# 128 of v's 1024 columns summed on VectorE for the first tile, h kept in two buffers, and the sample's selection and a second staging rearranged

## What is computed

```python
    h = x + mix
    hn = rmsnorm(h, norm_ffn_w)
    y = h + peer(hn.reshape(bsz * t, D_MODEL), peer_w_q, peer_sub_keys, peer_u, peer_v).reshape(bsz, t, D_MODEL)
...
        sv, si = lax.top_k(sc, PEER_TOPK)
        cand = sv[:, :, 0, :, None] + sv[:, :, 1, None, :]
...
        fv, fi = lax.top_k(cand.reshape(PEER_BLOCK, PEER_HEADS, PEER_TOPK * PEER_TOPK), PEER_TOPK)
...
        gate = jax.nn.softmax(fv, axis=-1)
        ue = u[eidx]
        ve = v[eidx]
        act = jax.nn.gelu(jnp.einsum('thkd,td->thk', ue, xb).astype(F32), approximate=False)
        return jnp.einsum('thk,thkd->td', (gate * act).astype(xb.dtype), ve)
```

## Time and profile before

| | |
|---|---|
| median of 3 runs | 3275.91 us |
| the profiled execution: own time | 3276.45 us |
| its span | 3274.7 us |
| TensorE busy | 2923.6 us (89%) |
| VectorE busy | 2114.2 us (65%) |
| GpSimd busy | 2074.2 us (63%) |
| ScalarE busy | 1532.2 us (47%) |
| moved by DMA | 1226.83 MB, mean 375 GB/s |
| the DMA engines' share | 0.9 or more in all but five of the 40 slices |
| of it, gathers (software queue) | 1121.46 MB |

### The profile page before, as it was taken

How to read it: one execution, slowest core, us unless ns; L and a number is a source line. 1 busy time by engine, 2 the same in 40 slices (tenths; PEclk the granted TensorE clock), 3 DMA queues, 4 the chain that set the end, 5 groups by cost and what they waited for, 6 DMA issues and landing times. The chain is left out here.

```text
span 3274.7 us, 31544 instructions
## 1 busy us (share of the span) xinstructions
PE 2923.6 (89%) x8213; PEld 1379.7 (42%) x8213; DVE 2114.2 (65%) x4852; ACT 1532.2 (47%) x4160; POOL 2074.2 (63%) x2162
## 2 busy tenths in 40 slices
PE   7998999879998999799988998899888997889966
PEld 6854544335443544354433443344334342343221
DVE  2465556656577656865667657875787477655684
ACT  3415642356336643475336643674358333633333
POOL 1105574766667676767667776777677776657675
PEclk9999999999999999999999999999999999989999
DMA  8518999999999999999999999999999999999998
GB/s 287 191 60 327 363 409 336 383 408 402 400 371 408 395 410 393 399 409 400 409 371 394 410 410 409 402 403 410 409 393 410 405 409 380 355 358 409 391 350 347
DMA packets 363485, 1226.83 MB, mean 375 GB/s; under 512 B 43259, under 2 KB 69852, under 8 KB 362012
## 3 DMA queue, kind: packets, MB, share of 16 engines
q0 software_dynamic: 308288, 1121.46, 87.4%
q1 hardware_dynamic: 27148, 70.75, 5.7%
q10 hardware_dynamic: 27872, 32.61, 2.9%
HBM read 1199.89 MB, written 25.79 MB: 374 GB/s over the span
## 5 line engine op out<-in xcount | busy, mean ns | idle before, releaser
L1196 PE MATMUL ps<-rows,diag 128*128 128x512 f32 (+1 forms) x4224 | 2021.8, 612 | 275.8 <-DMA rows<-in_peer_v,idx 186.2
L1619 DVE CUSTOM_DVE_ANT_0 rows<-rows,ps 128x1024 f32<-128x1024 f32 x1056 | 1267.3, 1215 | 602.9 <-DMA rows<-in_peer_u,idx 592.0
L567 POOL DMA_INDIRECT rows<-in_peer_v,idx x1056 | 1026.3, 972 | 568.2 <-PE ps L1196 345.5
L555 POOL DMA_INDIRECT rows<-in_peer_u,idx x1056 | 1022.8, 969 | 513.7 <-issue 274.4
L1196 PEld LDWEIGHTS ps<-rows,diag 128*128 128x128 f32 (+1 forms) x4224 | 767.2, 191 | 1367.4 <-issue 1067.9
L836 ACT ACTIVATE act_g<-act_g 128x1 f32<-128x1 f32 x1056 | 210.8, 200 | 988.2 <-DVE act_g L1619 974.6
L842 ACT ACTIVATE diag<-ident,act_g 128x128 f32<-128x128 f32 x1024 | 411.2, 402 | 357.4 <-PE ps L1196 331.3
L838 ACT ACTIVATE act_g<-act_g,gate 128x1 f32<-128x1 f32 x1056 | 311.0, 294 | 34.3
L1078 PE MATMUL ps<-w_sc,r 128*128 128x512 f32 (+1 forms) x576 | 288.1, 595 | 1.7 <-ACT r L752 1.7
L950 PE MATMUL ps<-rows,bias 128*128 128x384 f32 (+1 forms) x544 | 186.1, 495 | 0.0
L1078 PEld LDWEIGHTS ps<-w_sc,r 128*128 128x128 f32 (+1 forms) x576 | 101.9, 181 | 148.9 <-issue 146.1
(11 more groups left out here) (285 smaller groups left out, 1932.5 us busy)
## 6 DMA issues: line engine op xcount, KB each, us to landing
bias<-in_w_in ACTq DMA_DIRECT2D x34, 512.0 KB, 6.7
rows<-in_peer_u,idx POOLq DMA_INDIRECT x1056, 10.0
rows<-in_peer_v,idx POOLq DMA_INDIRECT x1056, 10.0
r<-proj SPq DMA_DIRECT2D x7, 1344.0 KB, 8.7
proj<-staged ACTq DMA_DIRECT2D x44, 192.0 KB, 5.0
w_sc<-in_w_q_t SPq DMA_DIRECT2D x8, 1024.0 KB, 8.5
rows<-in_w_in POOLq DMA_DIRECT2D x14, 512.0 KB, 4.0
w_o<-in_w_in POOLq DMA_DIRECT2D x10, 512.0 KB, 6.8
```

What stands on the lines that cost most here:

```text
L555: nc.gpsimd.indirect_dma_start(ring[:, slot, :], None, a["peer_u"], bass.IndirectOffsetOnAxis(ap=idx[g % 2][:, k:k + 1], axis=0), engine_s ...
L567: nc.gpsimd.indirect_dma_start(ring[:, slot, :], None, a["peer_v"], bass.IndirectOffsetOnAxis(ap=idx[g % 2][:, k:k + 1], axis=0), engine_s ...
L1196: last = nc.tensor.matmul(Y[j][0:m, :], diag[:, n % DIAGS, 0:m], ring[:, slot, 512 * j:512 * (j + 1)], start=(k == 0), stop=(k == steps_of ...
L1619: V.tensor_tensor_reduce(ring[:, slot, :], ring[:, slot, :], hn_u, 1.0, 0.0, ALU.mult, ALU.add, col).then_inc(S["dots"], 1)
```

## The change

Three parts go in together.

- **Side sum.** For tile 0 alone, VectorE adds up columns 0 to 127 of the v rows itself, into `side_acc` (gate[1]), one scalar_tensor_tensor per row, three steps behind the dot. TensorE's first matmul then has 384 columns. A v slot is free once both have read it. Because gate[1] is taken, tile 1's gates are first written elsewhere and copied at step 4 of period 1.
- **h in two buffers.** `resid[0]` and `resid[1]` take the place of `hx` and `hn`; h is no longer stored and reloaded. The transposes for the scores start from h itself; the ffn norm's weight is multiplied in when VectorE copies them out of PSUM, rstd when ScalarE copies the scores. hn_u is h x rstd x weight in one VectorE operation. The weights lie in a ring slot for tile 0 and in r3 after, loaded once the selection is done. The finish of a tile moves to later steps (`finish_steps`).
- **Sample and staging.** The sample's scores go to four groups of 32 partitions, two heads each, so that the selection covers 128 partitions with two heads. `TIMES_SAMPLE` is written anew. The prologue's odd blocks are staged in ring slot 7. SyncE issues the first two state loads earlier.

```diff
+SIDE, SIDE_LAG, GATES_AT_HAND = P, 3, 8
...
-    t = {MIX: mix, TURN: mix + 1, SCALED: mix + 2, SUMMED: summed, SQUARED: summed + 1, NORMED: summed + 2,
-         NORM_TURN: summed + 3, NORM_KEPT: summed + 4, CAND: cand, PLACES: cand + 1, SPLIT: split, GATE: split + 2, PICK: pick}
+    t = {MIX: mix, TURN: mix + 1, SCALED: mix + 2, SUMMED: summed, SQUARED: summed + 1, NORM_TURN: summed + 1,
+         NORM_KEPT: summed + 2, NORMED: summed + 3, CAND: cand, PLACES: cand + 1, SPLIT: split, GATE: split + 2, PICK: pick}
...
-TIMES_SAMPLE = {k: k - 20 for k in range(60)} | late_times(
-    41, lambda c: 44 + c, 61, lambda c: 66 + c, lambda g: 74 + 8 * g, lambda g, x: 75 + 8 * g + (3 if g < 2 else 2 if g < 3 else 1) * x,
-    101, lambda j: 102 + 2 * j, 110, 111, 117)
+TIMES_SAMPLE = {1: -24, 5: -22, 2: -18, 4: -15, 6: -13, 7: -12, 10: -11, 9: -10, 11: -8, 12: -6, 13: -4, 14: -2, 17: -1, 15: 0,
+                18: 2, 16: 3, 19: 4, 20: 6, 21: 8, 22: 10, 23: 13} | {k: k - 15 for k in range(26, 60)} | late_times(
+    46, lambda c: 49 + c, 66, lambda c: 72 + 3 * c // 4, lambda g: 97, lambda g, x: 98 + x,
+    100, lambda j: 102, 104, 105, 112)
...
+    return (2, 3, 4) if w >= TILES - 1 else (2, 12, 19) if w + 2 == TILES else (2, 27, 34) if w + 2 < 3 else (2, 6, 13)
...
-        hn = sb("hn", [P, D])
-        hx = sb("hx", [P, D])
+        resid = [sb(f"resid{n}", [P, D]) for n in range(2)]
...
+        side_acc = gate[1][:, :]
+        gate_raw = [r3[:, 896:1024] if f == 1 else gate[f % 2] for f in range(TILES + 1)]
+        gate_out = [r2[:, 0:PICKS] if f == 1 else gate[f % 2] for f in range(TILES + 1)]
...
+        staged_odd = rows[:, 7 * D:7 * D + PASS3]
...
+        w_ffn = [rows[:, 14 * D:15 * D] if f == 0 else r3[:, :] for f in range(TILES + 1)]
+        w_fin = r2[:, D:2 * D]
...
+            sp.dma_start(w_ffn_t, a["norm_ffn"][0, :].rearrange("(c p) -> p c", p=P), allow_slow_non_contiguous=True).then_inc(S["consts_in"], 16)
...
+            def load_w_ffn(f):
+
+                sp.wait_ge(S["topk_done"], f + 1)
+                sp.dma_start(w_ffn[f], a["norm_ffn"]).then_inc(S["w_ffn_in"], 16)
...
-                    sp.dma_start(h_at, hx[0:ntok(f), :]).then_inc(S["h_stored"], 16)
-                    sp.wait_ge(S["h_stored"], 16 * f + 16)
-                if g is not None:
-                    if f is not None:
-                        sp.wait_ge(S["hn_ready"], f + 1)
-                    sp.dma_start(hx[0:ntok(g), :], h_dram[SEQ:TOK, :] if is_sample(g) else h_tiles[g])\
-                      .then_inc(S["h_back"], 16)
...
+                if use == 1 and slot == 14:
+                    pool.wait_ge(S["hn_taken"], 1)
+                if use == 1 and slot == 7:
+                    pool.wait_ge(S["proj_out_odd"], stores_before(len(BLOCK_AT[-1]), True))
                 if earlier is not None:
                     pool.wait_ge(S["vsum"], earlier + 1)
+                    if earlier < PICKS:
+                        pool.wait_ge(S["side_sum"], earlier + 1)
...
-                if b:
-                    act.wait_ge(S["proj_out"], stores_before(b))
+                odd = odd_first(b)
+                out, out_s = (staged_odd, staged_s_odd) if odd else (staged[:, :], staged_s)
+                stored = S["proj_out_odd"] if odd else S["proj_out"]
+                if stores_before(b, odd):
+                    act.wait_ge(stored, stores_before(b, odd))
...
+                        nc.scalar.activation(sc[:, 4 * g:4 * g + 4, :], F[SCORE_BANK[g]].rearrange("p (c t) -> p c t", c=4),
+                                             ACT.Copy, scale=rstd).then_inc(S["sc_kept"], 1)
...
+                    out = F[SCORE_BANK[0]][NS * g:NS * (g + 1), :] if is_sample(f) else F[SCORE_BANK[g]]
...
                 for j in range(2):
-                    last = nc.tensor.matmul(Y[j][0:m, :], diag[:, n % DIAGS, 0:m], ring[:, slot, 512 * j:512 * (j + 1)],
+                    lo = SIDE if g == 0 and j == 0 else 0
+                    last = nc.tensor.matmul(Y[j][0:m, lo:512], diag[:, n % DIAGS, 0:m], ring[:, slot, 512 * j + lo:512 * (j + 1)],
                                             start=(k == 0), stop=(k == steps_of(g) - 1))
...
+                        last = V.tensor_tensor(hn_t[:, 4 * j:4 * j + 4, 0:n],
+                                               F[j][:, 0:4 * n].rearrange("p (c t) -> p c t", c=4),
+                                               w_ffn_t[:, 4 * j:4 * j + 4].unsqueeze(2).to_broadcast([P, 4, n]), ALU.mult)
...
+            def side(k):
+
+                slot, _, use = V_SLOTS[k]
+                dve.wait_ge(S["diag_ready"], k + 1)
+                dve.wait_ge(row_in[slot], 16 * use)
+                col = act_g[:, k % ACTS:k % ACTS + 1]
+                part = ring[:, slot, 0:SIDE]
+                if k == 0:
+                    V.tensor_scalar(side_acc, part, col, None, ALU.mult).then_inc(S["side_sum"], 1)
+                else:
+                    dve.wait_ge(S["side_sum"], k)
+                    V.scalar_tensor_tensor(side_acc, part, col, side_acc, ALU.mult, ALU.add).then_inc(S["side_sum"], 1)
...
                     if g is not None and k < steps_of(g):
                         dot(g, k)
+                    if g == 0 and k >= SIDE_LAG:
+                        side(k - SIDE_LAG)
...
-                        V.tensor_copy(hn_u, hn[:, :]).then_inc(S["hn_taken"], 1)
+                        V.scalar_tensor_tensor(hn_u, resid[f % 2][:, :], rstd, w_ffn[f], ALU.mult, ALU.mult)\
+                            .then_inc(S["hn_taken"], 1)
```

301 lines of the change are left out of this document (167 added, 134 removed).

## The result

The changed kernel takes 3229.15 us, the median of 4 runs (3224.76 to 3231.33), beside 3277.10 us (4 runs, 3273.2 to 3280.58; the forecast started from the first three of them, 3275.91) for the kernel before: a ratio of 0.9849, 95% interval 0.9833 to 0.9865, or 48 us less. The forecast was 3229, with a range of 3198 to 3262.

The account below looks back on a forecast made before the run. Transfers at 408 GB/s were taken to bound clean periods, other engines the slower ones. Terms 18.9 + 10 - 3 + 1 + 11 + 9 = 46.9 us off 3276.45 gave 3229.5, stated as 3229 us, range 3198 to 3262.

Parts of the forecast that it names:

- What bounds the kernel: Clean periods such as period 4 (343 us) are bound by transfers at 408 GB/s; there only fewer bytes help.
- Bytes, 18.9: Periods 0 to 7: h is no longer stored and reloaded, 1.285 us per 512 KB transfer, net 18.9 us saved.
- Period 0, 10 and 3: Period 0: 128 columns moved off TensorE gain 10 us (48 steps x 0.215); VectorE's side sums cost 3 us.
- The rule of the Trainium skill: VectorE instructions with two SBUF inputs contend with GpSimd instructions reading SBUF; the second blocks until the first is done.
- the rival: Period 0: side sums lengthen most gathers, costing 13 to 26 us without the 10 gained; 3252, at most 3265; 15 in 100.
- Prologue, 1: Prologue: two stagings remove ScalarE's store waits and VectorE's 3.11 us wait; 1 us counted, between 4.5 gained and 3 lost.
- End of period 6, 11: Last sixteen steps of period 6: the sample's attention, spread by the new table, wins 11 of 13.0 us lost.
- Selection, 9: Period 7: the sample's selection on four groups of 32 rows wins 11 us, less 2 for denser scores: 9 us.
- States, 0: Period 7: the chain of the sample's eight state loads and stores, and its cost, stay as they are.
- the third rival: More than counted: TensorE's 22 us come whole, the prologue gives 4.5, the samples all 27; 3206; 14 in 100.
- Slower: Period 0: VectorE and TensorE walk in step; with half of VectorE's work not overlapping, 481 us, total 3321; 5 in 100.
- new waits of TensorE for ScalarE's diagonals: Sign of the second rival, first 20 steps of period 7: sample's 20 us shrink to 5; 3244; 18 in 100.

## Why the prediction was right, point by point

- **The sum.** The forecast of 46.9 us is met to 1 us, and that is partly luck. Periods 0 to 5, and period 6 without its end, gave 4.5 us more than forecast; the end of period 6 and the sample's selection gave 4 less.
- **What bounds the kernel.** Right on the first chip: the clean periods 4 and 5 stay at 405 to 406 GB/s and became 1.9 us shorter each, of 2.57 for the bytes taken out. On chips A and B transfers alone don't bound either kernel; no row of the first chip could have told that.
- **Bytes, 18.9.** Right, by the 2.4 to 2.5 us that are missing at the very steps of the store and the reload. Periods 1 to 5 gained 14.6 us, 1.7 more than the bytes; periods 2 and 3, with 4.4 and 4.6, gave it, in their first sixteen steps (5.0 and 3.4), and why these got faster was not looked into. The added copies neither confirmed nor refuted the term, on chips where bytes alone don't bound.
- **Period 0, 10 and 3.** Right to 2 us in sum. Steps 80 to 111 gained 0.20 us each. How much of the 11.5 us is the side sum's was measured on chip A alone: 4.5. The price was taken too high. The side sum itself is longer than my row (0.35 for 0.29) and still costs nothing: the kernel that pays it and has no gain is no slower. GpSimd lost 1.3 us to it, where I had 1.
- **The rule of the Trainium skill** ("SBUF — State Buffer", "Who interferes with whom"). The trace bears out the rule, but not the price that I made of it for the rival. A gather of v, and the two-tensor operation that had begun 0.81 us before it:

```profile
587.75 2.28 POOL L602 DMA_INDIRECT rows<-in_peer_v,idx  x1 [1.94 <-PE ps L1249]
...
586.94 2.28 DVE L1527 TENSOR_TENSOR r<-r,small 128x2048 f32<-128x2048 f32 x1
```

1.47 us were left of VectorE's operation when the gather began, and 1.47 + 0.81 = 2.28. The same holds for the 3.04 us of rows 8 (2.23 left, + 0.81), and for every gather of the changed kernel's trace that took over 1.1 us beside such an operation of 0.6 us or more, 45 of them: what is left, plus 0.81 us. Five gathers that began within 0.03 us of the operation's start were not held and took 0.94, which is what a gather takes alone. So a side sum of 0.35 us can hold one up by 0.35 + 0.81 - 0.94 = 0.22 us at most, which is an estimate from these durations; 0.12 was the most measured, and 0.02 the mean of the 69. The rival took 0.10 to 0.20 us in every step.
- **Prologue, 1.** Right in sum (0.6), partly wrong in detail. The 3.11 us wait of VectorE for the exponentials did not go (it is 3.06 now): ScalarE stands in order and comes to them only behind a block and a table load of 1.28 us. The wait for the odd store came as said, 2.39 us of GpSimd's at 278.95 us.
- **End of period 6, 11.** Near in size (8.7 us net), with a cause that the runs don't bear out. "TensorE waits 9.33 us for k_t" was named first as the cause. Putting the wait back, at 14.72 us, cost nothing that the periods show. The links of the chain, one step apart, brought the long window of 37.4 us back; what they cost in the end stays between 7 us by the windows, which the spread of such windows doesn't confirm, and 12 to 16 by the ratios. That the second chain behind the first makes the rest was not tried. I also took 11 of 13 us lost by the rate, without saying that the end gains 20.1 and the start of the next period gives 11.4 back. The table by period is off by 10 and 13 us mostly for that reason.
- **Selection, 9.** Nearly right in sum, 7.0 us in steps 72 to 127, but not where I had put it. The three windows that I priced gave 6.2 us for 9, steps 72 to 95 gave 5.5 that no row had promised, and the last eight took 4.6 back. What was given back for the scores is VectorE's wait of 11.59 us; the run with scores in 32 steps moved that loss and did not remove it.
- **States, 0.** Right in sum: steps 16 to 71 of period 7 took 164.5 us and take 164.0. But this is the largest loss that is left, and spreading it, with SyncE's new order, gave 11 us by the medians and 12 to 14 by the period.
- **Slips in the text.** The range's lower end, 3198, isn't worked out; the third rival ends at 3206. Its upper end, 3262, counts 26 us in place of the 3 already in the sum, where the rival itself says at most 3265. "Slower" is reached once 36% and not 39% don't overlap. TensorE is late in "all 104 steps" in one place and in steps 24 to 103, 80 steps or 17 us, in another. None of these moves the forecast.
- **Rivals.** None came. The side sums did not eat period 0. Of the sample's gain 11.4 us went back at the start of period 7, but as rows no longer in hand, not as new waits of TensorE for ScalarE's diagonals in the first 20 steps (4.7 us there before, 6.5 now). VectorE and TensorE did not walk in step in period 0.

## What to carry to other kernels

Read a gain over the boundary of a stage, not inside one stage: work that is late leaves landed data behind, and the next stage runs faster than the bound until that is used up. Begin the count at one dot and end it at one dot, so that the wait at the boundary itself is in it. Do not price a wait by its own length: the periods show no loss behind a wait of 14.72 us of TensorE, because it does its adds faster (2.33 us) than the rows come (2.57). A chain over three engines with one step between the links did hold sixteen steps up, 37.4 us for 21.2 in the first eight. An operation of a third of a microsecond on the engine with slack may be put beside another engine's descriptor work; ask how long the overlap with a lock can last (0.22 us here), not only how often there is one.
